# Output projection of a two-layer mixed-attention trunk: from plain float32 products to three products of split operands

## The reference, cut to what matters

```python
def token_mixing(h, p, ctx):
    ...
    out = jnp.concatenate([o_a, o_b, o_c, o_d], axis=-1) @ p['w_out']
    ...
def trunk_layer(x, mod, p, ctx):
    ...
    u, state = token_mixing(h, p, ctx)
    x = layer_norm(ALPHA * x + gate[:, :, 1] * u, p['ln_g'][1], p['ln_b'][1])
```

## Time and profile before

| | |
|---|---|
| median of 3 runs | 3079.4 us (3075.28 to 3079.95) |
| the profiled execution | 3075.94 us |
| its span, first to last instruction | 3074.1 us |
| mean granted TensorE clock | 0.977 of full speed |
| TensorE busy with products | 2922.6 us, 95% |
| VectorE busy | 1290.2 us, 42% |
| ScalarE busy | 904.9 us, 29% |
| transfers | 259 MB, mean 84 GB/s |

### The profile page before, as it was taken

How to read it: one execution, slowest core, us unless ns; L and a number is a source line. 1 busy time by engine, 2 the same in 40 slices (tenths; PEclk the granted TensorE clock), 3 DMA queues, 4 the chain that set the end, 5 groups by cost and what they waited for, 6 DMA issues and landing times.

```text
span 3074.1 us, 46411 instructions
## 1 busy us (share of the span) xinstructions
PE 2922.6 (95%) x20109; PEld 2595.9 (84%) x20109; DVE 1290.2 (42%) x1815; ACT 904.9 (29%) x1262; POOL 35.2 (1%) x32
## 2 busy tenths in 40 slices
PE   6999999998999899999979999999999998999997
PEld 5999998776755599999979999977776657999996
DVE  3223225436663622323542322364376636233236
ACT  3222222323452422122252222233235514222222
POOL 0000000100000000000000000001000000000000
PEclk8999999999998999999989999999999989999998
DMA  9222334104120322322532232331142113213211
GB/s 310 69 61 84 82 115 131 55 14 122 57 90 14 110 69 65 89 72 84 157 110 78 59 90 76 115 109 55 28 138 73 45 28 105 74 57 88 82 57 54
DMA packets 359017, 259.03 MB, mean 84 GB/s; under 512 B 27152, under 2 KB 310100, under 8 KB 358740
## 3 DMA queue, kind: packets, MB, share of 16 engines
q1 hardware_dynamic: 358868, 256.85, 27.6%
HBM read 253.25 MB, written 3.57 MB: 84 GB/s over the span
## 4 chain that ended last, share of the span: by engine, by line
PE 89%; DVE 7%; ACT 1%; issue 1%; DMA 1%; SPq 1%; DVEq 0%; ACTq 0%
PE banks L743 57%; PE banks L653 17%; PE banks L603 1%; PE banks L1029 1%; PE banks L1224 1%; PE banks L1203 1%; PE banks L857 1%; DVE x_res L1848 1%; PE banks L1239 1%; PE banks L1196 1%; DVE w_split L1728 1%; PE banks L923 1%; PE banks L908 1%; DVE softmax_cols L2143 1%; PE banks L1205 0%
## 5 line engine op out<-in xcount | busy, mean ns | idle before, releaser
L743 PE MATMUL banks<-h_hi,w_split 128*128 128x320 f32 x5376 | 1185.1, 309 | 2.1 <-DVE mod L1677 2.1
L743 PEld LDWEIGHTS banks<-h_hi,w_split 128*128 128x128 f32 x5376 | 899.2, 188 | 2.9 <-issue 2.9
L743 PE MATMUL banks<-h_lo,w_split 128*128 128x320 f32 x2688 | 830.9, 309 | 0.0
L743 PE MATMUL banks<-hid_hi,w_split 128*128 128x320 f32 x2816 | 624.0, 310 | 0.1
L1728 DVE TENSOR_TENSOR w_split<-w_slots,w_split 128x2048 fp32r<-128x2048 f32 x152 | 348.4, 2292 | 421.5 <-ACT w_split L1288 421.5
L1288 ACT ACTIVATE arena<-banks 128x640 f32<-128x640 f32 (+8 forms) x336 | 170.9, 536 | 1198.6 <-PE banks L743 886.6
L743 PEld LDWEIGHTS banks<-h_lo,w_split 128*128 128x128 f32 x2688 | 504.7, 188 | 0.0
L743 PEld LDWEIGHTS banks<-hid_hi,w_split 128*128 128x128 f32 x2816 | 471.7, 188 | 1.7 <-issue 1.2
L743 PE MATMUL banks<-hid_lo,w_split 128*128 128x320 f32 x1408 | 435.2, 309 | 0.0
L1288 ACT ACTIVATE w_split<-w_slots 128x2048 fp32r<-128x2048 f32 x152 | 290.2, 1909 | 403.7 <-PE banks L743 397.0
L1792 DVE TENSOR_TENSOR arena<-arena,banks 128x640 f32<-128x640 f32 x88 | 72.2, 821 | 751.3 <-ACT arena L1288 751.3
(11 more groups left out here) (261 smaller groups left out, 2373.0 us busy)
## 6 DMA issues: line engine op xcount, KB each, us to landing
w_slots<-in_ffn_w_gu SPq DMA_DIRECT2D x176, 512.0 KB, 5.2
arena<-in_w_mod SPq DMA_DIRECT2D x14, 2048.0 KB, 12.6
w_slots<-in_ffn_w_down SPq DMA_DIRECT2D x64, 384.0 KB, 3.7
w_slots<-in_ffn_w_down SPq DMA_DIRECT2D x64, 320.0 KB, 4.3
h_mod<-in_w_mod SPq DMA_DIRECT2D x8, 2048.0 KB, 8.1
w_slots<-in_w_mod SPq DMA_DIRECT2D x8, 2048.0 KB, 9.1
mixed<-in_w_mod SPq DMA_DIRECT2D x6, 2048.0 KB, 9.2
w_slots<-in_w_in SPq DMA_DIRECT2D x6, 2048.0 KB, 7.8
```

The costliest lines, as they stand in the source:

```text
L743: ins = mm(banks[:, b0 + hf, 0:HALF], w[:, k, :], x[:, k, t], start=w is wlo and k == 0, stop=w is whi and x is hi and k == kt - 1, skip_g ...
```

## The change

The output projection works on split operands as the feed-forwards do.

- The result is split in eleven parts (`MIX_PARTS`): the six whole tiles 2, 3, 4, 5, 0, 1 and the five groups of attention D. ScalarE copies a part to the high tiles (six in the memory of `h_hi`, two in `hid_lo`), VectorE subtracts it in place. Ten parts stand within the attention loop, behind the units in `MIX_AT`; the last part, the last group, follows the loop.
- Each output tile's weights (128 x 1024) are split likewise: high part to one of four places in the arena, low part in place in the slot. Tiles 0 and 1 stand within the attention loop (`OUT_AT`), 2 and 3 behind it, 4 to 7 one by one as tiles 0 to 3 are done.
- Each output tile is made of 2 halves x 8 k-steps x 3 products over 320 tokens. For o0 the k-steps of tiles 6 and 7 come last and wait for the last part.
- `residual` takes a tile in three pieces (320, 192, 128 tokens) where it took two (512, 128).
- Modulation 12's weights go to a part of the arena where `h_mod` held them, and are fetched behind modulation 14's, when five groups are copied.

The two tables and new functions, and the core of the loops:

```diff
+OUT_K = (2, 3, 4, 5, 0, 1, 6, 7)
...
-            MOD_AT[l, 12], MOD_AT[l, 14] = hmod[:, 0:SLOT], arena[:, 0:SLOT]
+            MOD_AT[l, 12], MOD_AT[l, 14] = arena[:, 9728:9728 + SLOT], arena[:, 0:SLOT]
...
+        MIX_PARTS = [(2, None), (3, None), (4, None), (5, None), (0, None), (None, 5), (1, None)] + [(None, g) for g in range(6, 10)]
+        MIX_AT = {5: 0, 8: 1, 11: 2, 14: 3, 24: 4, 26: 5, 27: 6, 30: 7, 34: 8, 38: 9}
+        OUT_AT = {28: 0, 32: 1}
...
                 fill("o0", [(w_slot("o0", 8, 512), w_out[:, :, 0:512])])
-                sp.wait_ge(s["side_done"], o["side_done"] + len(SIDE))
-                fill_mod(l, 12)
...
                 sp.wait_ge(s["new_ready"], o["new_ready"] + 1)
                 fill_mod(l, 14)
+                sp.wait_ge(s["on_used"], o["on_used"] + len(units) // 8)
+                fill_mod(l, 12)
                 sp.dma_start(a["out_ckv"][0, l], NEWROWS[:, 0:P]).then_inc(s["small_store"], 16)
...
                 for m in range(KT_M):
-                    if m % 4 == 0:
-                        weights(f"o{m // 4}")
-                    run(f"o{m}", w_slot(f"o{m // 4}", 8, 512), (m % 4) * P, P, MIX, 8)
+                    j = job[f"o{m}"]
+                    slot_free(j)
+                    pe.wait_ge(s["out_lo"], o["out_lo"] + m + 1)
+                    whi, wlo = OUT_HI[m % 4], out_cols(m)[1]
+                    order = [(b, k) for b in range(2) for k in OUT_K]
+                    if m == 0:
+                        pe.wait_ge(s["mix_lo"], o["mix_lo"] + 7)
+                        order = [x for x in order if x[1] < 6] + [x for x in order if x[1] >= 6]
+                    for i, (b, k) in enumerate(order):
+                        if m == 0 and i == 12:
+                            pe.wait_ge(s["mix_lo"], o["mix_lo"] + 11)
+                        _, t0, n = HALVES[b]
+                        for w, x in ((wlo, MIX_HI[k]), (whi, MIX_LO[:, k]), (whi, MIX_HI[k])):
+                            ins = mm(banks[:, slot(j) + 2 * b, 0:n], w[:, k, :], x[:, t0:t0 + n], start=w is wlo and k == OUT_K[0],
+                                     stop=k == OUT_K[-1] and w is whi and x is MIX_HI[k], skip_group_check=True)
+                    ins.then_inc(s["done"], 1)
...
+                def mixed_hi(i):
+                    tile, g = MIX_PARTS[i]
+                    if g is None and tile >= 2:
+                        act.wait_ge(s["mixed_ready"], o["mixed_ready"] + 2)
+                    else:
+                        act.wait_ge(s["on_used"], o["on_used"] + (5 if g is None else g + 1))
+                    plain, hi, _ = mix_part(i)
+                    f(hi, plain).then_inc(s["mix_hi"], 1)
+
+                def out_hi(m):
+                    at, n = number[f"o{m // 4}"]
+                    act.wait_ge(w_loaded[at], o["w_loaded"][at] + loaded_at[at][n])
+                    if m in (2, 3):
+                        act.wait_ge(s["on_used"], o["on_used"] + len(units) // 4)
+                    if m >= 4:
+                        act.wait_ge(s["done"], o["done"] + job[f"o{m - 4}"] + 1)
+                    f(OUT_HI[m % 4], out_cols(m)[0]).then_inc(s["out_hi"], 1)
...
                     if u + 2 < len(units):
                         probs(u + 2)
+                    if u in MIX_AT:
+                        mixed_hi(MIX_AT[u])
+                    if u in OUT_AT:
+                        out_hi(OUT_AT[u])
+                mixed_hi(len(MIX_PARTS) - 1)
+                for m in range(2, KT_M):
+                    out_hi(m)
...
-                    for g, (b, t0, n) in enumerate(SEGS):
-                        ins = v.scalar_tensor_tensor(out=X[:, m, t0:t0 + n], in0=group_cols(j, b, n), scalar=MOD[:, sub, 2, m, g:g + 1],
+                    for src, t0, n, g in ((banks[:, slot(j), 0:HALF], 0, HALF, 0), (banks[:, slot(j) + 2, 0:LAT - HALF], HALF, LAT - HALF, 0),
+                                          (banks[:, slot(j) + 2, LAT - HALF:HALF], LAT, CTX, 1)):
+                        ins = v.scalar_tensor_tensor(out=X[:, m, t0:t0 + n], in0=src, scalar=MOD[:, sub, 2, m, g:g + 1],
...
+                def mixed_lo(i):
+                    plain, hi, lo = mix_part(i)
+                    dve.wait_ge(s["mix_hi"], o["mix_hi"] + i + 1)
+                    v.tensor_tensor(lo, plain, hi.bitcast(F32), ALU.subtract).then_inc(s["mix_lo"], 1)
+
+                def out_lo(m):
+                    plain, lo = out_cols(m)
+                    dve.wait_ge(s["out_hi"], o["out_hi"] + m + 1)
+                    v.tensor_tensor(lo, plain, OUT_HI[m % 4].bitcast(F32), ALU.subtract).then_inc(s["out_lo"], 1)
...
+                    if u - 2 in MIX_AT:
+                        mixed_lo(MIX_AT[u - 2])
+                    if u - 2 in OUT_AT:
+                        out_lo(OUT_AT[u - 2])
+                mixed_lo(len(MIX_PARTS) - 1)
+                out_lo(2)
+                out_lo(3)
                 for m in range(KT_M):
                     residual(f"o{m}", 1, m)
+                    if m < 4:
+                        out_lo(m + 4)
```

More of the change, by code:

```diff
@@ L190, in per_layer @@
              sin_ready=1, fin_out=2, ft_turned=1, ft_ready=1, y_ready=1, ysq=1, y_rstd=1,
[L191 removed]
+             excl_zero=1, f_raw=4, f_ready=4, mixed_ready=2, mix_hi=11, mix_lo=11, out_hi=8, out_lo=8, aq_sq=3, aq_rstd=2, aq_norm=2,
              akv_norm=1, cache_turned=1, cache_ready=1, rot_done=8, rot_used=8, roped=8, kcopied=2,
@@ L249, in trunk_kernel @@
         HLO = rsb("h_lo", KT_M * TOK)[:].rearrange("p (k t) -> p k t", k=KT_M)
-        rsb("raw_gap", SLOT)
+        raw_gap = rsb("raw_gap", SLOT)
         w_split0 = rsb("w_split0", 2 * RAW)
-        HIDHI = rsb("hid_hi", FG * TOK)[:].rearrange("p (k t) -> p k t", k=FG)
-        HIDLO = rsb("hid_lo", FG * TOK)[:].rearrange("p (k t) -> p k t", k=FG)
+        hid_hi, hid_lo = rsb("hid_hi", FG * TOK), rsb("hid_lo", FG * TOK)
+        HIDHI, HIDLO = (x[:].rearrange("p (k t) -> p k t", k=FG) for x in (hid_hi, hid_lo))
         w_split1 = rsb("w_split1", 2 * RAW)
@@ L327, in trunk_kernel, with mix_part, out_cols @@
         XIN = view(0, 5, D_MODEL)
+        MIX_HI = [HHI[:, i] for i in range(6)]
+        MIX_HI_D = HIDLO[:, 0:2]
+        MIX_HI += [MIX_HI_D[:, i] for i in range(2)]
+        MIX_LO = HLO
+        OUT_HI = [x.rearrange("p (k c) -> p k c", k=8) for x in (
+            hid_lo[:, 1280:2304], w_split1[:, 0:1024], hid_hi[:, 4096:5120], hid_hi[:, 5120:6144])]
+        OUT_LO = [x[:, 0:SLOT].rearrange("p (k c) -> p k c", k=8) for x in (raw_gap, w_split0)]
+        MIX_PARTS = [(2, None), (3, None), (4, None), (5, None), (0, None), (None, 5), (1, None)] + [(None, g) for g in range(6, 10)]
+        MIX_AT = {5: 0, 8: 1, 11: 2, 14: 3, 24: 4, 26: 5, 27: 6, 30: 7, 34: 8, 38: 9}
+        OUT_AT = {28: 0, 32: 1}
+        def mix_part(i):
+            tile, g = MIX_PARTS[i]
+            if g is None:
+                return MIX[:, tile], MIX_HI[tile], MIX_LO[:, tile]
+            cols = slice(units[4 * g]["q"], units[4 * g]["q"] + P)
+            return MIX[:, 6:8, cols], MIX_HI_D[:, :, cols], MIX_LO[:, 6:8, cols]
+        def out_cols(m):
+            name, cols = f"o{m // 4}", slice((m % 4) * P, (m % 4 + 1) * P)
+            return w_slot(name, 8, 512)[:, :, cols], OUT_LO[number[name][0]][:, :, cols]
         def cc(name, rows=P):
@@ L354, in trunk_kernel @@
                  "cs_done cs_used sin_zero sin_ready fin_out ft_turned ft_ready "
-                 "y_ready ysq y_rstd excl_zero f_raw f_ready mixed_ready "
+                 "y_ready ysq y_rstd excl_zero f_raw f_ready mixed_ready mix_hi mix_lo out_hi out_lo "
                  "aq_sq aq_rstd aq_norm akv_norm cache_turned cache_ready rot_done rot_used roped kcopied "
@@ L1247, in _ @@
                 for m in range(KT_M):
-                    if m % 4 == 0:
-                        weights(f"o{m // 4}")
-                    run(f"o{m}", w_slot(f"o{m // 4}", 8, 512), (m % 4) * P, P, MIX, 8)
+                    j = job[f"o{m}"]
[14 more added lines that the diff above has]
+                    ins.then_inc(s["done"], 1)
+                    dense_count[0] = j + 1
                     if m % 4 == 3:
```

1 line of the change is left out of this document (removed).

## The result

| | before | after |
|---|---|---|
| median of 4 runs | 3077.9 us (3075.28 to 3079.95) | 3050.8 us (3050.35 to 3051.10) |
| span of the profiled execution | 3074.1 us | 3049.3 us |

The ratio is 0.9915, 95% interval 0.9902 to 0.9928: 27.0 us less, where 26.6 were forecast and 3051 us were named. Ratios go by fast executions; one of 9063 us (of the version with 512 and 128 columns) and one of 3318 us (of the kernel before), both slow, are left out. The sum was right to half a microsecond. Not all of its terms were, as the profile shows.

The account below looks back on a forecast made before the run. TensorE was taken to bound the kernel; 13.8 - 0.3 - 0.2 = 13.3 us less per layer, 26.6 for both, gave 3049.3 from the profile and 3052.8 from the median; forecast 3051 us, range 3041 to 3062.

Parts of the forecast that it names:

- The projection's own time: Output projection: 48 products at 0.1462 us, 7.02 us per tile; 58.8 us against 72.6, 13.8 us less per layer.
- the columns rival: Output projection: only columns count, 0.133 us per product, 6.4 us per tile; total 3040 us; chance 5%.
- the part I left open: Projection's products at full clock: something besides columns sets part of the spacing, 0.146 us measured where columns give 0.133.
- The half clock in the projection: Projection's start: clock rises 5.9 us in as before; 22 products at 0.267 instead of 0.146 us lose 2.7 us.
- Splitting in the loop: Attention loop: ten parts and two weight tiles fit mostly in idle gaps; 0.3 us lost per layer, bounds 0 to 17.2.
- a sign against me: Attention loop: TensorE idle before transposes released by VectorE's scaling would show the forecast wrong; no size given.
- the slower rival: Attention loop: all 17.2 us of inserted work delay TensorE, layer 3.6 us longer, 3083.1 us; chance 4%.
- VectorE behind o4: Projection after the mean product: o5's residual ends at 13.6 us, o7 needs its bank at 15.1; slack 1.5, no cost.
- Weight tiles: Projection: splitting tiles 2 to 7 meanwhile is hidden; tile 2 is ready after 4 us, needed some 16 us in.
- the eleventh part: Projection's start: the last group's copy and subtraction take 0.84 us, hidden behind over 7 us of o0's other products.
- the moved transfer: Modulation 12's weights (2 MB), fetched after the fifth attention group: 8.1 us to landing, 100 available; no cost.
- The residual: Projection's end: three pieces of 0.54, 0.41 and 0.34 us against 1.01; 0.2 us more per layer, counted in full.

Follow-up runs that it names:

- 512 and 128 columns: Changed kernel with the projection's products over 512 and 128 tokens instead of twice 320, residual in two pieces: 3066.5 us (0.9960).
- two products: Changed kernel without the projection's product of the weights' low part, all splitting still done: 3014.6 us (0.9795).
- a few cheap products in the waits: Three unused identity transposes before those of units 32 to 39, added to two rearranged versions of the changed kernel: 3044.1 us (0.9901) and 3043.3 us (0.9894).
- splitting behind the loop: Changed kernel with all eleven parts and all weight tiles split after the attention loop, none within it: 3063.5 us (0.9960).
- no three in a row: Changed kernel with attention A's tiles split earlier, nothing behind unit 27, and the second weight tile split after the loop: 3050.3 us (0.9920).
- the stall: Changed kernel with all splitting after the attention loop, plus three VectorE subtractions into spare memory behind iterations 29 and 30: 3064.0 us (0.9961).
- everything twice: Changed kernel with every splitting copy and subtraction within the attention loop made twice, weight tiles included: 3066.8 us (0.9970).

## Why the prediction was right, point by point

- **The projection's own time**: right, and for the reasons given. 7.04 us per tile against 7.02, 58.6 us against 58.8. With two products the tile takes 4.69 us, so the price per product is the same in the projection as in the feed-forwards, and the columns rival (0.133 us) falls. The experiment with 512 and 128 columns gives the size of the part I left open, not its cause: 13 ns on top of 320 or 512 columns, and more than twice the columns' time at 128. TensorE: Matmul & The Clock Gate (Back-to-back issue gap) of the Trainium skill gives, for an isolated product, the columns' time at 2.4 GHz and 2.5 ns, 216 ns at 512 columns and 56 at 128; for these products, each with its own weights, 226 and 114 ns were measured, and the measurement decides.
- **The half clock in the projection**: mis-sized. I let it last 5.9 us, as before; it lasted 3.9 (965.54 to 969.5), the clock having fallen later. Kept at full clock, the stretch is 1.8 us shorter than the changed kernel's (62.4 against 64.2), where I had 2.7 us for it. Eight tiles of 7.04 us and 1.8 are 58.1 of the 58.6 us measured; the other 0.5 lies in tenths around the first tile, the pause, the mean product and the end of the last product, which I did not count.
- **Splitting in the loop**: the cost was small, as I said, but twice what I took (0.57 us against 0.3) and wrong in place. I followed each late subtraction alone and judged each to have slack. Units 5 and 11 cost nothing, as I said; the neighbours at iterations 29 and 30 did, and TensorE's waits for the scaling, which I had named as a sign against me, rose from 2.9 to 4.6 us. Two steps failed: taking the gaps one by one, and taking the long gap of units 8 to 11 (1.75 us before an odd unit's maximum) for attention D as well, where it is 1.21 us before unit 33's.
- **The clock in the loop**: missing from the sum. I wrote that more idle time might bring the half clock forward, as help for the slower rival. The opposite came: the fall moved from 77.4 to 84.3 us into the loop, units 34 to 37 ran at full clock, and 2.0 us came back, 1.4 net per layer. With my sign for it, attention within 0.5 us of 88.6, that term is plainly missed: the loop is 1.4 us shorter, and I had excluded a gain. That the change brings the later fall is shown by the loops in which it came or did not; how it does is not (last section).
- **VectorE behind o4**: right. 1016.45 against an end of o6 near 1018.5 leaves 2 us where I had 1.5; the two-product run hits this bound at the computed place with 2.73 us.
- **Weight tiles, the eleventh part, the moved transfer, the parameter loads**: no wait, as forecast. **The residual** in three pieces takes 1.14 us against 1.01; from the first product behind the projection (1025.80; before 1038.05) to the normalization it is 3.45 us against 3.34, 0.1 us where I counted 0.2.
- **Outside the projection**: I had nothing. The third to the fourth normalization takes 0.9 us more in both profiles of the changed kernel, and between 0.2 and 1.2 more in every variant, although nothing in that stretch was changed. The granted clock goes with it. It rises 23.2 us behind the third normalization in the kernel before and 25.1 in the changed kernel, and over all fourteen profiles the stretch is the longer the later that rise: 501.9 us at 23.2, 502.1 at 23.7 (two products), 502.5 at 24.6, 502.8 at 25.1, 503.2 at 26.0 (512 and 128 columns). From the fourth normalization to the second layer's first unit it is the same: 345.0 us where the clock falls 6.0 us in, 345.3 at 6.3, 345.9 at 7.1, 346.1 at 7.6. So most of this loss goes with the clock. Why its change comes at another place there was not tested and stays open.

So the total was right partly by luck. In the first pair of profiles 4.0 us more were gained than I counted, 3.2 were lost outside and 2.6 in start-up, and the medians lie 2.2 us further apart than the profiles' spans: 26.6 + 4.0 - 3.2 - 2.6 + 2.2 = 27.0.

## What to carry to other kernels

Price a reformulated matmul by the start-to-start distance of the same form at the same clock, not by counting cycles per column: float32 takes four here (8.65 us for 8 x 640 columns) and a reduced product at half clock one, which would make three of them 75% of float32; they cost 81%, and at 128 columns the gain is gone. Work for an engine with idle gaps is free as long as each gap is longer than what is put in and no late step meets the next one; look at pieces in consecutive iterations together. Where the granted clock falls within a stage that keeps TensorE waiting, the clock is a term of the sum like any other, and a few cheap products in the waits were worth more here than the work they took.

## What the runs showed of the hardware that was not expected

The granted clock's fall moved with shifts of half a microsecond. With TensorE's loop undelayed (kernel before, splitting behind the loop, no three in a row: eight loops) it fell 9.6 to 10.8 us ahead of the last copy in all, and in two of them came back for 3 us. With unit 32 late by 0.57 us, and the loop otherwise nearly the same (twelve loops), it fell 1.4 to 2.7 us ahead of the last copy in eleven and not at all in one. A longer delay did not do the same: with unit 32 late by 1.6 us (the stall) it fell 13.8 us ahead for 3 us, with 4.2 us (everything twice) 17 us ahead for good. What preceded the earlier fall was no long wait. The window of the kernel before ahead of it:

```profile
943.00:953.00 10.00, 9.01 (x73) 6.21 (x71) 6.93 (x26) 5.71 (x18) 0.00 (x0) 0.98 0.00 1
```

TensorE was busy for 9.0 of 10 us, and in its timeline from 940 to 953 one row alone lists idle time that another engine ended:

```profile
952.32 0.74 PE L1239 MATMUL banks<-cst,arena 128*128 128x128 f32 x3 [0.87 <-DVE arena L2160]
```

Nor was it a low busy share that told the two apart: in the changed kernel the clock held from 953.0 to 962.5 with TensorE busy for 6.7 of 9.5 us. What a short delay changes in TensorE's pattern so that the clock holds is not settled by these runs. That it holds with more products in the waits is shown by four loops of four, the small delays that come with them not separated.
